# Packing the experts of a two-layer MoE decoder step into 14 instead of 15 row slots, with shared slots cut at 96 columns

## The reference

```python
def hier_moe(x, g2, r_g, r_e, w_gate, w_up, w_down):
    h = rmsnorm(x, g2).reshape(b * t, d)
    gi = jnp.argmax(softmax(h @ r_g), axis=-1)        # one of 4 groups
    tw, ti = lax.top_k(softmax(le_sel), 2)            # two of its 4 experts
    ...
    a = jax.nn.silu(hg) * hu * gates[..., None]       # per expert: D 1024 -> 2*256
    return jnp.einsum('nef,efd->nd', a, w_down)       # 256 -> 1024, gated sum
```

## Time and profile before

| what | value |
|---|---|
| median of 3 runs | 1098.41 us (1096.93 to 1098.92) |
| the profiled execution's own time | 1098.67 us |
| its span | 1097.0 us |
| mean granted TensorE clock | 0.972 |
| TensorE busy | 998.4 us (91%) |
| VectorE / ScalarE / GpSimd busy | 423.5 / 236.7 / 194.9 us |
| moved by DMA | 197.69 MB, mean 180 GB/s |

### The profile page before, as it was taken

One profiled execution on the slowest core, in us unless ns is written; L12 is line 12 of the kernel. 1 busy time (PEld: TensorE's weight loads), 2 busy tenths in 40 slices (PEclk: granted clock), 3 DMA queues, 4 the chain that ended last, 5 costly groups with the idle time before them and its releaser, 6 DMA issues.

```text
span 1097.0 us, 13030 instructions
## 1 busy us (share of the span) xinstructions
PE 998.4 (91%) x4666; PEld 514.9 (47%) x4666; DVE 423.5 (39%) x1084; ACT 236.7 (22%) x483; POOL 194.9 (18%) x269
## 2 busy tenths in 40 slices
PE   7999998989998989999589999989989899899992
PEld 4434464546455434454344344645555464344440
DVE  2402123356357445412233211234473573662123
ACT  2111354432001110111211114554210011111110
POOL 2323102121001110111115031121120011111200
PEclk9999999999999998999889999999999999999996
DMA  9606013323305788997542050233151067899755
GB/s 348 241 1 239 1 45 115 109 84 122 138 30 207 283 325 296 408 337 281 206 140 77 30 211 1 90 92 127 47 195 72 32 268 270 314 369 395 260 202 201
DMA packets 40199, 197.69 MB, mean 180 GB/s; under 512 B 8064, under 2 KB 8192, under 8 KB 24256
## 3 DMA queue, kind: packets, MB, share of 16 engines
q1 hardware_dynamic: 19600, 136.21, 32.4%
q0 software_dynamic: 16464, 45.88, 12.1%
q10 hardware_dynamic: 4064, 14.68, 3.6%
HBM read 178.39 MB, written 30.93 MB: 191 GB/s over the span
## 4 chain that ended last, share of the span: by engine, by line
PE 80%; DVE 7%; DMA 5%; issue 3%; ACT 3%; POOL 1%; POOLq 0%; ACTq 0%; DVEq 0%; SPq 0%
PE ps L652 73%; PE ps L650 6%; DMA hT<-h_rows,igat 3%; DMA par<-in_par 1%; DVE st L1480 1%; PE ps L667 1%; DMA cat<-y_rows 1%; ACT ring L1208 1%; DMA y_rows<-hn,isca 1%; DVE hT L1364 1%; DVE tmp L1508 1%; DVE st L1509 1%; POOL st L496 0%; ACT L1208 0%; DVE o_sb L1500 0%
## 5 line engine op out<-in xcount | busy, mean ns | idle before, releaser
L652 PE MATMUL ps<-ring,hT 128*128 128x512 f32 (+1 forms) x1008 | 395.0, 601 | 14.9 <-DVE hT L1364 5.4
L652 PEld LDWEIGHTS ps<-ring,hT 128*128 128x128 f32 (+1 forms) x1008 | 157.6, 177 | 214.5 <-issue 203.1
L652 PE MATMUL ps<-ring,cat 128*128 128x512 f32 (+1 forms) x480 | 202.6, 596 | 8.9 <-ACT ring L1221 3.4
L652 PEld LDWEIGHTS ps<-ring,cat 128*128 128x128 f32 (+1 forms) x480 | 77.1, 178 | 95.1 <-issue 88.4
L1821 DVE TENSOR_TENSOR hT<-ps,par 128x512 f32<-128x512 f32 x60 | 38.6, 685 | 117.4 <-PE ps L650 117.0
L596 POOL DMA_INDIRECT y_rows<-hn,isca x30 | 30.0, 1001 | 298.4 <-ACT hn L1277 269.1
L652 PE MATMUL ps<-hT,ring 128*128 128x512 f32 (+1 forms) x256 | 71.8, 437 | 0.3 <-ACT cat L1171 0.3
L494 POOL TENSOR_SCALAR st<-st 128x1 f32<-128x1 f32 (+3 forms) x60 | 15.9, 265 | 305.8 <-ACT sqj L1127 109.7
L496 POOL TENSOR_TENSOR st<-st,half 128x1 f32<-128x1 f32 (+3 forms) x60 | 62.9, 1049 | 11.0 <-POOL st L494 10.1
L1480 DVE TENSOR_REDUCE st<-ps 128x2 f32<-128x256 f32 (+3 forms) x32 | 26.3, 823 | 97.2 <-PE ps L652 96.8
L1277 ACT COPY hn<-ps 128x1024 f32<-128x1024 f32 x30 | 30.4, 1012 | 128.2 <-PE ps L652 128.2
(11 more groups left out here) (248 smaller groups left out, 1144.4 us busy)
## 6 DMA issues: line engine op xcount, KB each, us to landing
ring<-in_w SPq DMA_DIRECT2D x86, 1024.0 KB, 8.9
kc<-in_w SPq DMA_DIRECT2D x10, 1024.0 KB, 9.1
vc<-in_w SPq DMA_DIRECT2D x10, 1024.0 KB, 9.7
v<-in_w SPq DMA_DIRECT2D x10, 1024.0 KB, 7.1
kc<-in_ck POOLq DMA_DIRECT2D x32, 256.0 KB, 3.6
vc<-in_cv POOLq DMA_DIRECT2D x32, 256.0 KB, 3.2
kva<-in_w SPq DMA_DIRECT2D x8, 1024.0 KB, 8.0
h_rows<-qk ACTq DMA_DIRECT2D x10, 512.0 KB, 2.6
```

What stands on the lines that cost most here:

```text
L652: ins = pe.matmul(out, lhsT, rhs, start=start, stop=stop, skip_group_check=loose)
```

## The change

Slots now have widths: a share is given as (position, first place, columns). A shared slot can be cut 96 to 32 or 64 to 64, so positions hold 160, 128, 96 or 64 rows, and there are 14 slots instead of 15. Three experts are not sorted. A share of 96 columns is made of a matmul with 64 columns and one with 32 (`columns`). The order is worked out later (by_size in turn 0, places_by_size in turn 1), the preparation of groups is spread over other turns, `EXTRA` grows from 8 to 12, and g1 gets its own buffer, loaded once at the start.

```diff
-EXTRA = 2 * (TP * P + NROW) // P - 1
-EXTRA += EXTRA % 2
+EXTRA = 12
-STILL = 2
+STILL = 3
-SLOTS = [[(0, 0)], [(1, 0)], [(2, 0)], [(2, P), (11, 0)], [(3, 0)], [(4, 0)], [(9, 0), (10, 0)], [(5, 0)], [(6, 0)], [(7, 0)], [(8, 0)],
-         [(12, 0)], [(12, P), (15, 0)], [(13, 0)], [(14, 0)]]
+SLOTS = [[(0, 0, 128)], [(1, 0, 128)], [(2, 0, 128)], [(3, 0, 128)], [(7, 0, 96), (3, P, 32)], [(4, 0, 128)], [(9, 0, 64), (10, 0, 64)], [(5, 0, 128)],
+         [(6, 0, 128)], [(11, 0, 64), (15, 0, 64)], [(8, 0, 96), (12, P, 32)], [(12, 0, 128)], [(13, 0, 128)], [(14, 0, 128)]]
...
-        GROUPS = [range(0, 1), range(1, 2), range(2, 4), range(4, 8), range(8, 12), range(12, NSLOT)]
+        GROUPS = [range(0, 1), range(1, 2), range(2, 3), range(3, 7), range(7, 11), range(11, NSLOT)]
...
-        INDEX_AT = {0: 2, 1: 3, 2: 4, 4: 5, 6: 6, 8: 7}
-        PLACES_AT = {5: 6, 7: 7}
+        INDEX_AT = {1: 3, 3: 4, 5: 5, 7: 6, 9: 7, 11: 8}
+        PLACES_AT = {1: 3, 3: 4, 5: 5, 6: 6, 8: 7, 10: 8}
...
+        LOW_AT = {LAST + 1: (0, 1), LAST + 2: (2, 3, 4)}
...
+        def columns(n):
+
+            out = []
+            for at, pos, _ in shares(n):
+                begin = at.start
+                for w in (P, P // 2, P // 4):
+                    if at.stop - begin >= w:
+                        out.append((slice(begin, begin + w), pos))
+                        begin += w
+            return out
...
+            sp.dma_start(g1_sb[:, :, :], d["g1"]).then_inc(*g1_in.inc(by=16))
...
                 index_rows(1)
-                keep_busy(16)
+                keep_busy(4)
+                index_rows(2)
+                keep_busy(12)
...
-                    dve.wait_ge(*par_in.at("par"))
-                    scaled, turned = norm_tile("h1", "rs1", "g1")
+                    dve.wait_ge(g1_in.sem, 16)
+                    scaled, turned = norm_tile("h1", "rs1", g1_sb[:, 0, :])
...
-                for g in range(2):
+                for g in range(STILL):
+                    if g == STILL - 1:
+                        early_hot(g)
                     hot(g, slice(TP - 1, TP), g)
                     index(g)
-                by_size()
+                logits_down()
                 in_turned(0, ("m", 0))
-                places_by_size()
-                logits_down()
                 for n in range(NSLOT):
...
+                    if n == 0:
+                        by_size()
+                    if n == 1:
+                        places_by_size()
```

More of the change, by code:

```diff
@@ L1006, in index_rows @@
                                 continue
-                            for at, pos, _ in halves(s):
+                            for at, pos in columns(s):
                                 mm(bank("I")[at, n * 4:n * 4 + 4], onehot[:, s % 4, t, at], rows_of[:, t, pos, :],
@@ L1027, in up @@
                     pe.wait_ge(*read[f"T{hf}"].at("tr", *key, hf))
-                    for _, i in parts:
+                    for i in dict.fromkeys(i for _, i in parts):
                         arrived(i)
@@ L1054, in weights @@
                 def weights(n, part):
-                    return [(at, PIECE_AT[pos, part]) for at, pos, _ in halves(n)]
+                    return [(at, PIECE_AT[pos, part]) for at, pos in columns(n)]
                 def free(number):
@@ L1283, in _ @@
                         silu(n % 2, ("m", n))
-                    if LAST < n < NSLOT:
+                    if n in LOW_AT:
                         for b in range(2):
                             act.wait_ge(*y_out[b].at("y", "m", last_slot(b, LAST)))
-                        for t in range(2 * (n - LAST) - 2, min(2 * (n - LAST), NT)):
+                        for t in LOW_AT[n]:
                             rows = NROW if t == TP else P
@@ L1396, in _ @@
                     constants()
+                dve.wait_ge(*par_in.at("par"))
                 dve.wait_ge(*ws_in.at("ws"))
@@ L1581, in _ @@
                     head_scale(t)
-                scaled, turned = norm_tile("h2", "rs2", "g2")
+                scaled, turned = norm_tile("h2", "rs2", par[:, PAR["g2"]])
                 flat = placed[:, :, :]
@@ L1723, in main_group @@
                     for s in GROUPS[g]:
-                        for at, pos, first in halves(s):
+                        for at, pos, first in shares(s):
                             ins = one_hot(s, at, placed_by[:, :, pos], first)
                     ins.then_inc(*dve_s.inc("onehot", g))
-                    index(g)
                 def extra_group(g):
@@ L1853, in _ @@
                         extra_plan()
+                    if n == 5:
                         late_gates()
+                    if n in INDEX_AT:
+                        index(INDEX_AT[n])
                     if n + 1 < NSLOT:
@@ L1857, in _ @@
                     gated(n % 2, ("m", n))
-                    for t in range(2 * (n - LAST) - 4, 2 * (n - LAST) - 2) if n >= LAST + 2 else []:
+                    for t in LOW_AT.get(n - 1, ()):
                         add_low(t)
-                add_low(TP)
+                for t in LOW_AT[NSLOT - 1]:
+                    add_low(t)
                 n_extra = extra_slots(dve, "dve")
@@ L1959, in layout @@
     for parts in SLOTS:
-        for pos, _ in parts:
-            c32[:, C_CAP][:, pos] += P // len(parts)
+        for pos, _, wide in parts:
+            c32[:, C_CAP][:, pos] += wide
     rows = np.zeros((P, NT, 4))
```

45 lines of the change are left out of this document (21 added, 24 removed).

## The result

The changed kernel takes 1130.41 us (median of 4 runs, 1127.74 to 1133.95) against 1098.66 us of the kernel before on the same chip: ratio 1.0291, 95% interval 1.0256 to 1.0326. It is slower by 2.9%, and 10.4 us above the forecast of 1120, outside its range. The profiled execution is the slowest of the four (1133.95 us, span 1132.2).

The account below looks back on a forecast made before the run. The prediction took the kernel as bound by TensorE's work, 73% of the span, and what makes it wait. Terms -37.8 + 54.5 + 5.6 = +22.3 on 1098.41 gave 1120.7, stated as 1120 us; range 1059 to 1128.

Parts of the forecast that it names:

- The cut slots (+54.5): Four slots cut at 96: TensorE empties at width changes, 1.13 us more per block, 12 blocks a slot, +54.5 us.
- both width terms: Width changes in the cut slots' expert products, +54.5 us, and in their `index_rows`, +5.6 us; together +60.1.
- Index width changes (+5.6): `index_rows` of cut slots: 5 tiles with two changes each, 4 x 10 x 0.14 us = +5.6.
- the term of +1.7: Index matmuls: 145 instead of 120 per layer at 0.034 us each, +1.7 us for both layers.
- Slot gone, overflow plan, slot 2's gather (-41.2): Expert stages: one slot less -22.8 us, no stop or slow rows at slot 5 -14.0, unsorted slot 2's gather -4.4.
- Places in turn 1 (+1.0): VectorE's places_by_size and one-hots in turn 1 end after TensorE reaches `index_rows`: +0.5 us per layer, +1.0.
- Before slot 0 (+2.4, "between 0.5 and 3"): Before slot 0: one-hot wait and two pieces loaded during the row store, +1.2 us per layer (0.5 to 3), +2.4.
- Norm factors (-5.0 + 2 = -3.0): Layer 1's start: no wait for `par` -2.5 us, faster rows behind it -2.5; pieces beside the last scatter +2.
- -37.8: Sum in us of all forecast parts of the change except the mixed column widths.
- The rival of widths side by side: In cut slots, 64- and 32-column products overlap, so +60.1 shrinks to perhaps +1: 1061.6 us, chance 0.26.

Follow-up runs that it names:

- kernel 1: The changed kernel with its two slots cut at 96 made of four 32-column products per block, in expert and index matmuls; 1072.84 us, ratio 0.9776.
- kernel 9: kernel 6 with the plan for overflow put back behind an `index`, in turn 5 instead of at the start of turn 4; 1073.72 us, ratio 0.9789.
- kernel 5: kernel 3 with the two weight pieces held until the rows of slot 0 are gathered, not only stored; 1061.38 us, ratio 0.9678.
- kernel 6: kernel 5 with the next layer's second weight piece also held until the last rows are read back; 1057.67 us, ratio 0.9648.
- kernel 8: The kernel before with the norm factors of both layers in their own buffer, loaded at the start; 1094.86 us, ratio 0.9983.
- kernel 4: The changed kernel with all 64-column products first, then those of 32, in each half of `up` and `down`; 1120.45 us, ratio 1.0211.
- kernel 2: The changed kernel with a layer's seventh and eighth expert pieces issued only once the rows h_rows are stored; 1127.94 us, ratio 1.0288.
- kernel 3: The changed kernel with the edits of kernel 1 and kernel 2 together; 1071.11 us, ratio 0.9756.
- kernel 11: kernel 6 with all of the next layer's weight pieces behind the first held until the last rows are read back; 1064.71 us, ratio 0.9702.
- kernel 7: The kernel before with two of three shared slots made of one 64-column and two 32-column products per block; 1138.51 us, ratio 1.0393.
- kernel 10: kernel 6 with the wait for `par` put back ahead of the second layer's first `turned`; 1058.93 us, ratio 0.9645.

## Why the prediction was wrong, point by point

- **The cut slots (+54.5): right, to the size.** 1.98 us a block against 1.99, and 57.6 us when both width terms are taken away (forecast 60.1).
- **Index width changes (+5.6): too high.** Against kernel 1, where the same two groups have 40 matmuls and take 0.96 and 0.86 us, the mixture costs 0.95 and 0.86 us, 3.6 in both layers. In turn the rate of 0.034 was too high: side by side, 40 take what I took for 25. All `index_rows` of a stage take 4.00 us in the kernel before and 4.30 in kernel 1, +0.3 where the term of +1.7 had 0.85 in each layer.
- **Slot gone, overflow plan, slot 2's gather (-41.2): right in kind.** No stop before slot 5 and no wait for a gather in turn 1; kernel 9 puts the plan at 16 us where I had 14. The slot alone I did not test.
- **Places in turn 1 (+1.0): nothing.** `index_rows` at 371.25 follows the rows before it at once. The index widths, the number of index matmuls and the places together are 2.05 of the 3.3 us by which each stage came in under the forecast; the rest I did not follow. That errors of this size have the other sign and hide part of the miss below is luck.
- **Before slot 0 (+2.4, "between 0.5 and 3"): this step failed.** I named the cause ("two weight pieces are now loaded while the rows for the gather are stored") and gave it, together with TensorE's wait for the one-hot of slot 2, 1.2 us in each layer with no row behind it. The stretch measured +5.61 and +3.40, and the slow first rows another 1.16 and 1.01. Kernel 5 against kernel 1 shows 11.5 us for both layers (10.8 by the ratios); in kernel 5 the stretch is back at 13.6 and 14.2 us, within 0.4 of the kernel before, so the other half of the term is next to nothing. What happens in layer 0 of the changed kernel: the store lands in 7.81 us, the gather is issued 12.8 us after the last turning of x instead of 7.6 (340.26), and the first rows run slower at the clock of 0.50. Both the bound and the value were too small: 1 MB takes 2.75 us at the rate of the earlier trace rows, and two of them run beside a store that everything waits for, an estimate of 5.5 a layer. The store took 5.2 us longer than the median 2.6 us of the kernel before in layer 0, and 3.8 longer in layer 1 (6.38).
- **Norm factors (-5.0 + 2 = -3.0): the second step that failed.** In the profiled execution of the changed kernel the first half came as forecast: the stop 1.09 instead of 4.22 us and the rows 5.39 instead of 7.91, -5.65. The second half was too small: the stop ahead of the fillers is 13.80 us instead of 9.82 behind the slower scatter, +3.98 where I took +2 (kernel 6 gives 3.3 to 3.7 for one piece). With 0.5 more at the first tile the stretch is -1.13 instead of -3.0. But taking half of the gain from the rows was a reading that does not hold: it goes by the clock, and with the same code kernel 1 ran them in 7.01 us behind a stop of 2.13. By the run of kernel 8 the whole change of buffer is worth -1.35 with zero inside the interval.
- **The clock.** The prediction took slow rows behind a stop as part of the stop's price and never named their cause, and it expected the clock at 1.00 in both stages. It was 0.50 from 350 to 356 us and again at 910 to 913.
- **Sum by the runs.** Apart from the widths I had -37.8; kernel 1, without them, is 24.3 us below the kernel before, so 13.5 us are missing. Before slot 0 are 8.4 to 9.1 of them (10.8 to 11.5, less 2.4), and the stretch at the layer's end, +0.85 in kernel 1's trace instead of -3.0, is 3.85.
- **The rest of the profiled execution.** It shows 2.8 and 3.0 us more in the two attention parts and 3.1 at the very end, which the prediction had at nothing. Two windows of the changed kernel (us, busy of PE, PEld, DVE, ACT, POOL, clock, DMA share, GB/s):

```profile
170.00:180.00 10.00, 8.56 (x39) 4.96 (x38) 3.96 (x13) 6.63 (x17) 1.38 (x3) 0.83 0.07 17
190.00:200.00 10.00, 6.81 (x17) 2.85 (x14) 5.50 (x17) 3.84 (x11) 5.89 (x9) 0.66 0.57 169
```

and of kernel 1, which is the same program up to this point:

```profile
170.00:180.00 10.00, 8.56 (x42) 4.79 (x41) 3.95 (x13) 6.63 (x17) 1.38 (x3) 1.00 0.07 16
190.00:200.00 10.00, 7.74 (x15) 3.52 (x16) 4.32 (x12) 3.45 (x8) 4.38 (x7) 0.83 0.40 127
```

The granted clock is 0.83 between 170 and 180 us in the changed kernel and in kernel 4, and 1.00 in the other twelve traces, kernel 1 among them. Kernels 1, 2 and 3 are the changed kernel up to this part and reach the last `c,x` turning of layer 0 at 332.09, 331.90 and 331.97 us, before the 332.65 of the kernel before. So the 2.8 us in layer 0 go with the execution and not with the change. The very end likewise: from the last turning to the end of the span it is 23.8 us here, 20.0 in kernel 1, 20.7 before and at most 22.1 in the others. The 3.0 us of layer 1 are of the same kind. The clock is 0.83 from 730 to 740 us and 0.66 from 750 to 760 here, and 0.94 and 0.89 from 730 to 750 in the kernel before, otherwise 1.00 between 600 and 860 us. The same stretch takes 311.7 to 316.4 us in the other traces, and in kernel 8, the kernel before but for one buffer, 314.92 against 312.04. That the profiled run lies 3.5 us above the median fits both, but which part of it is in the median stays open.

The rival of widths side by side was wrong, but its number (1061.6) is what kernels 5 and 6 reach (1061.4, 1057.7) when one width is used and the transfers are kept apart. That the two agree is in part luck, since terms of both signs in the -37.8 were off. Kernel 6 is the fastest: 3.5% below the kernel before and about 6% below the changed one.

## What to carry to other kernels

Where products lie side by side in TensorE, give them one column width in the whole block: here four of 32 cost what one of 128 costs, and 64 with 32 and 32 costs 2.3 times as much. Keep large loads away from a transfer that everything waits for (the store, the gather, the last scatter). Holding such a load one step too short only moves the collision to the next transfer, and holding too many makes them late themselves (kernel 11). When a forecast names such a collision, price it with the bytes in front of it and not with a guess. And when rows run slower than the same rows elsewhere, read the granted clock of that window before their price is put down to a wait.

## What the runs showed of the hardware that I had not expected

- Row-number matmuls of 4 columns: 40 of them with cut slots of one width take 0.96 and 0.86 us, 35 with mixed widths 1.72 and 1.91 us.
- The twelve first rows of layer 1 take 5.39, 7.08 or 7.91 us. They took 5.39 behind stops of 1.09 and 2.75 us (changed kernel, kernel 7), with a granted clock of 1.00 in these rows; 7.08 behind 2.00 and 2.27 (kernels 8 and 10), with 0.50 in part of them (553 to 556 us in kernel 8); and 7.91 behind 4.22, with 0.50 from 555 to 561 us. So the length of the stop just before does not decide it alone.
- One program does not get one clock: from 170 to 180 us it was 0.83 in the changed kernel and 1.00 in kernels 1 to 3, which are the same up to there.
- The index-driven transfers of 128 rows named above land in 6.7 to 8.1 us where the loads were not held (first gathers of kernels 2 and 3, last scatters of layer 0 in the changed kernel and kernels 1 to 5). They land in 3.1 to 5.2 us with fewer loads or none beside them (last scatters of layer 0 in the kernel before and in kernels 6, 9, 10 and 11, first gathers of the kernel before and of the changed kernel).
